# One TensorE-bound kernel on one core: a small tile moved in on-chip memory, and the padding after it five columns wider

## The reference

```python
# first block
h  = modulate(rmsnorm(x, norm1_g), shift1, scale1)
u, v, val, gate = split(h @ w_in + b_in)
y_a = spatial_gating_mixer(gelu(u), gelu(v), ...)      # per-head 128x128 causal mixing
y_b = conformer_conv_mixer(val, gate, ...)             # width-31 depthwise convolution, group norm
x  = x + gate1 * (concat(rmsnorm(y_a), rmsnorm(y_b)) @ w_out)
h2 = modulate(rmsnorm(x, norm2_g), shift2, scale2)
x  = x + gate2 * ((silu(h2 @ Wg) * (h2 @ Wu)) @ w_ffn_out)
x  = modulate(rmsnorm(x, norm_f_g), shift_f, scale_f)
# second block, two layers: attention (forgetting + native sparse), then a pooling mixer,
# each with h = h + rmsnorm(mixer(rmsnorm(h))) and
# h = h + rmsnorm((silu(u @ w_gate) * (u @ w_up)) @ w_down)
```

## Time and profile before

| | |
|---|---|
| median of 3 runs | 1819.37 us (1818.94, 1819.37, 1823.51) |
| the profiled execution, its own time | 1818.94 us |
| span from its first to its last instruction | 1817.2 us |
| granted TensorE clock, mean over the span | 0.967 of full |
| PE busy | 1705.4 us, 94% |
| DVE, ACT, POOL busy | 914.7, 657.6, 182.5 us |
| moved by DMA | 179.73 MB, mean 99 GB/s |

### The profile page before, as it was taken

One profiled execution on the slowest core, in us unless ns is written; L12 is line 12 of the kernel. 1 busy time (PEld: TensorE's weight loads), 2 busy tenths in 40 slices (PEclk: granted clock), 3 DMA queues, 4 the chain that ended last, 5 costly groups with the idle time before them and its releaser, 6 DMA issues.

```text
span 1817.2 us, 22072 instructions
## 1 busy us (share of the span) xinstructions
PE 1705.4 (94%) x8153; PEld 1341.7 (74%) x8153; DVE 914.7 (50%) x1368; ACT 657.6 (36%) x937; POOL 182.5 (10%) x178
## 2 busy tenths in 40 slices
PE   1899899999999989999999899999999899999996
PEld 1667678888888766666657688888888688888885
DVE  6865684543333371555656644444435744444323
ACT  1324334444322241354555444443224433333221
POOL 5001119910000040000000000000200000000000
PEclk9999889999999989999999899999998799999998
DMA  7655154523322241111102122323222032233221
GB/s 283 208 187 169 43 189 157 185 98 103 105 96 95 74 107 47 59 36 36 36 25 69 57 95 92 104 92 118 96 75 81 12 104 92 94 102 114 96 79 46
DMA packets 49111, 179.73 MB, mean 99 GB/s; under 512 B 5984, under 2 KB 6656, under 8 KB 48928
## 3 DMA queue, kind: packets, MB, share of 16 engines
q1 hardware_dynamic: 44896, 166.75, 27.2%
q0 software_dynamic: 3008, 10.59, 2.0%
q10 hardware_dynamic: 1152, 1.66, 0.3%
HBM read 173.56 MB, written 2.10 MB: 97 GB/s over the span
## 4 chain that ended last, share of the span: by engine, by line
PE 67%; issue 22%; DVE 8%; ACT 2%; DMA 1%; POOL 1%; ACTq 0%; DVEq 0%; POOLq 0%; SPq 0%
PE bank L332 15%; PE bank L334 15%; PE bank L333 15%; PE bank L1195 3%; PE bank L1197 2%; PE bank L1196 2%; PE bank L1299 2%; PE bank L1255 2%; PE bank L1275 1%; PE bank L1037 1%; DVE ada_acc L1652 1%; PE bank L1180 1%; PE bank L1353 1%; DMA raw<-in_ada_w 1%; ACT w_hi L267 1%
## 5 line engine op out<-in xcount | busy, mean ns | idle before, releaser
L271 DVE TENSOR_TENSOR w_lo<-raw,w_hi 128x1024 fp32r<-128x1024 f32 (+1 forms) x236 | 322.3, 1366 | 656.6 <-ACT w_hi L267 656.4
L332 PE MATMUL bank<-h_hi,w_hi 128*128 128x512 f32 x1232 | 489.3, 397 | 4.9 <-DVE h_lo L519 1.5
L333 PE MATMUL bank<-h_lo,w_hi 128*128 128x512 f32 x1232 | 482.7, 392 | 0.0
L334 PE MATMUL bank<-h_hi,w_lo 128*128 128x512 f32 x1232 | 482.5, 392 | 0.0
L267 ACT ACTIVATE w_hi<-raw 128x1024 fp32r<-128x1024 f32 (+1 forms) x236 | 265.3, 1124 | 560.0 <-PE bank L334 493.8
L332 PEld LDWEIGHTS bank<-h_hi,w_hi 128*128 128x128 f32 x1232 | 233.1, 189 | 64.5 <-issue 7.3
L334 PEld LDWEIGHTS bank<-h_hi,w_lo 128*128 128x128 f32 x1232 | 233.1, 189 | 49.1
L333 PEld LDWEIGHTS bank<-h_lo,w_hi 128*128 128x128 f32 x1232 | 233.3, 189 | 47.9 <-issue 1.0
L332 PE MATMUL bank<-hid_hi,w_hi 128*128 128x512 f32 x528 | 205.5, 389 | 0.0
L334 PE MATMUL bank<-hid_hi,w_lo 128*128 128x512 f32 x528 | 205.4, 389 | 0.0
L333 PE MATMUL bank<-hid_lo,w_hi 128*128 128x512 f32 x528 | 205.4, 389 | 0.0
(11 more groups left out here) (325 smaller groups left out, 1939.2 us busy)
## 6 DMA issues: line engine op xcount, KB each, us to landing
raw<-in_f2i SPq DMA_DIRECT2D x88, 512.0 KB, 3.2
raw<-in_ffi SPq DMA_DIRECT2D x44, 512.0 KB, 3.3
raw<-in_f2o SPq DMA_DIRECT2D x32, 704.0 KB, 4.0
ada_w<-in_ada_w SPq DMA_DIRECT2D x32, 512.0 KB, 4.0
raw<-in_att_w SPq DMA_DIRECT2D x24, 512.0 KB, 3.2
raw<-in_ffo SPq DMA_DIRECT2D x16, 704.0 KB, 4.0
raw<-in_ada_w SPq DMA_DIRECT2D x16, 512.0 KB, 4.6
raw<-in_w_in SPq DMA_DIRECT2D x16, 512.0 KB, 5.3
```

The lines of the kernel that those rows point to most:

```text
L271: nc.vector.tensor_tensor(WL[par][:, 0:kc * P], RAW[s][:, 0:kc * P], WH[par][:, 0:kc * P].bitcast(F32), ALU.subtract).then_inc(wlo, 1)
L332: pe_.matmul(bank[:, :], w_h, hi[:, k0 + k, :], start=start and k == 0, stop=False)
L333: pe_.matmul(bank[:, :], w_h, lo[:, k0 + k, :], start=False, stop=False)
L334: last = pe_.matmul(bank[:, :], w_l, hi[:, k0 + k, :], start=False, stop=stop and k == kc - 1)
```

## The change

```diff
@@ -95,12 +95,12 @@
         HL = sb("h_lo", [P, C, S], F32R)
         TMP = sb("tmp", [P, 2, S])
         TMP2 = sb("tmp2", [P, 2, S])
-        IDN = sb("ident", [P, P])
         VEC = sb("vec_sb", [P, NVEC])
         MOD = sb("mod", [P, 64])
         GS = sb("gs", [P, 3, C])
         PG = sb("pool_gs", [P, C])
         CACT = sb("c_act", [P, C])
+        IDN = sb("ident", [P, P])
         ONE = sb("ones", [P, P])
@@ -115,7 +115,7 @@
-        PAD = sb("pad_to_row", [P, 16])
+        PAD = sb("pad_to_row", [P, 21])
```

## The result

| | before | after |
|---|---|---|
| median of 10 runs | 1820.04 us (1817.81 to 1823.51) | 1833.09 us (1827.41 to 1837.05) |
| ratio, 95% interval | | 1.0072 [1.0057, 1.0086] |
| span of the profiled execution | 1817.2 us | 1835.1 us |
| granted clock, mean | 0.967 | 0.963 |

The change costs 0.72%, 13.1 us (10.4 to 15.7 by the interval). It is slower than the forecast of 1819.8 us by 13.3 us, and inside the range of 1816 to 1845.

What follows compares the result with a forecast made beforehand. The prediction took PE's matmul pace as the bound. It put +0.4 us on the moved fp32r streams and 0 on all else, carried to the median of 1819.37 us: 1819.8 us, range 1816 to 1845 us.

Steps and rivals of the forecast that it cites:

- 1776 matmuls concerned: fp32r matmuls with a moved moving operand: 1584 in the down projections, 192 in the attention's output projection; 402.6 us of PE time.
- The edits put at nothing: Weight loads from moved tiles, elementwise work, the identity and transfers: cost 0, with bounds -0.5 to +0.5 us for the first two.
- The signs named for it: Down projection starts 0.2267 us apart if the forecast holds, 0.234 to 0.240 under R1; h streams at 0.2267 in every case.
- R1: Moving reads in down and output projections fetched in 64-byte pieces from their own start: 12.6 to 23.6 us slower, chance 0.33.
- (a): fp32r matmuls with a moved moving operand, in down and output projections: between 0 and 361 us more, +0.4 us taken.
- the row nearest in kind: Convolution's float32 matmuls on shifted `y_shifted` against aligned `conv`: both 0.43 us apart, so a shifted start was taken as free.
- The upper bound drawn from it: A shifted fp32r stream needs at most float32's 0.43 us a matmul, up to 361 us more over 1776 matmuls.
- 12.6 us (17 cycles): Lower price of R1: one whole piece of 17 cycles, 7.1 ns, added to each of the 1776 matmuls.
- The rule of 16-byte lines: SBUF has 16-byte lines and full speed needs two hits on a line, so a 32-byte shift changes nothing: zero for (a).
- R2: A straddling piece in the moved fp32r streams takes two whole fetches, pace towards float32's: up to 2180 us, chance 0.05.
- R3: Between phases, a stretch of PE at half clock falls away: 6.7 us faster, 1813 us, chance 0.06.
- R4: The change is inert and addresses count for nothing: 1819.4 us, counted with the forecast, together 0.52.

Runs made afterwards that it cites:

- ident_only: The kernel before with only the identity tile moved behind the small tiles and the padding kept at 16 columns: 1821.38 us, ratio 0.9998.
- all_shifted: The kernel before with an unused 32-byte tile ahead of everything, so all tiles, the weights' too, start 32 bytes later: 1820.59 us, ratio 0.9997.
- the first bench: A separate kernel of matmul streams alone, sweeping the moving operand's start, with rows 2176 bytes apart by turns: 230.0 ns a matmul from an aligned start run again.
- hid_back: The kernel after with 96 unused bytes ahead of the hid tiles, which start at multiples of 128 again: 1835.85 us, ratio 1.0068 to before.

## Why the prediction was right in its range and wrong in its number

**The frame held.** PE bound, 1776 matmuls concerned, all on the path, every cycle worth 0.74 us: 16 cycles make 11.8 us, and 10.4 to 15.7 were measured. The edits put at nothing (weight loads, elementwise work, transfers, the identity) were nothing within the intervals: `ident_only` at 0.9998, and `all_shifted`, which moves all of these operands too, at 0.9997. The signs named for it were the right ones: h streams stayed, hid streams went to 0.2333 where R1 had 0.234 to 0.240, and a down projection to 123 us where R1 had 127.

**The step that failed** is the choice between the ends in (a): "I take the first, +0.4 us, because the row nearest in kind, the shifted `y_shifted` against the aligned `conv`, shows no price at all". The term put at +0.4 us measured 11.8 (6.67 ns a matmul). That row could not show it. Float32 is free of it at each of the four distances tried (429.2 ns), so its silence said nothing on fp32r; the prediction named this doubt and still gave the forecast 0.52. The upper bound drawn from it held, but by a wide margin. The range held because it was widened to take in R1, with its 0.33; and since R1's own mechanism is wrong, that its price covered the result is in part luck.

**The mechanism given for R1 was wrong too**, though its price came near. It read the earlier trace rows as a loss of one cycle for 64 bytes, and so made "modulo 64" the variable. The benches contradict a loss per column: 352 cycles for 320 columns, 416 for 384, 544 for 512, each 32 more than columns, where one in 16 would give 340, 408 and 544. A fixed fee is not the whole rule either, with 280 cycles for 256 columns in the first bench and 486 for 448. What the earlier trace rows gave was the distance from a pair of fp32r matmuls side by side, on 64 rows each, to a line of another type, and not the pace of a stream: 0.17 us at 128 columns, where a stream of 128 columns runs at 111.7 ns (268 cycles). And the variable is the distance to the weights' start modulo 256, not the start by itself: `all_shifted` has every fp32r operand off a multiple of 64 and loses nothing, `hid_back` has its hid tiles at multiples of 256 and loses it all. That 12.6 us (17 cycles) stood beside the measured 16 is a coincidence.

**The rule of 16-byte lines**, cited from the Trainium skill, page "Advanced Engine Details and Errata", section "Memory Cachelines", would have made the term zero. By that rule and by the row chosen the time came out the same, and both missed: a shift by two whole such lines costs 6.67 ns a matmul here.

**R2, R3, R4**: no stream came near the float32 pace; no execution of after came under 1827.41 us; and addresses do count, so R4, which the forecast carried with it, is out.

## What to carry to other kernels

Before calling a change of layout inert, find the tightest stream and compare its operands' places with each other, not with round numbers: here the moving rows and the weights of fp32r matmuls of 128 x 512 want the same remainder modulo 256 bytes, and most other remainders cost 2 to 3% of the pace (64 bytes off 1%). A padding tile that looks useless may hold that remainder, and it has to be recomputed whenever a tile ahead of it changes. And what costs nothing in a stream at half the pace, here float32, can still cost something at full pace, here fp32r.

## What the hardware showed that I had not expected

- The pace of fp32r matmuls of 128 x 512 depends on the distance between the two SBUF operands modulo 256 bytes, where both keep their remainders from one matmul to the next: 226.7 ns at 0, 228.9 at 64, 229.2 at 60, 230.0 or 233.3 at 48, 231 to 235 at the others tried, 236.9 at 4 bytes. It doesn't depend on the absolute place (226.7 with both 32 bytes later).
- Over one cycle a column fp32r took 32 cycles more at 512 columns; bfloat16 took 6 more (518), and float32 6 over two cycles a column (1030).
- With 64 or 32 stationary columns an fp32r matmul at distance 0 takes 230.0 and 231.7 ns: slower than with 128 (226.7).
- The extra isn't there at every length: 384 columns took 173.3 ns and 320 took 146.7 ns at distance 0 and at 32 alike, 448 took 202.7 and 206.7.
- 128 moving columns cost 111.7 ns and 256 cost 116.7 ns in the first bench: 128 columns less saved 5 ns there, where they save 53 between 512 and 384 (226.7 and 173.3). So at 128 the moving stream is probably not what takes the time.
